# One block for the mixer and the output projection of a hybrid layer, on one Trainium2 core

## The reference, cut to what matters

```
y      = ssd_chunked(xs, dt, A, Bm, Cm) + d_skip * xs          # (512, 16, 64)
y_ssm  = rms_norm(y * silu(z), ssm_norm_w)                      # (512, 1024)
y_att  = rms_norm(forgetting_attention(q, k, v, log_f), attn_norm_w)
y_mix  = concatenate([y_ssm, y_att], axis=-1)                   # (512, 2048)
out    = einsum('bsk,kd->bsd', y_mix, w_out)                    # (512, 1024)
x      = layer_norm(ALPHA * x + (1 + g1) * out, ln1_g, ln1_b)
rms_norm(x, w): x * rsqrt(mean(x * x) + 1e-5) * w
```

## Time and profile before

| | us |
|---|---|
| runs | 2349.56, 2351.22, 2354.84 |
| profiled execution, span | 2351.2 |
| PE busy | 2251.0 (96%) |
| DVE busy | 879.8 (37%) |
| ACT busy | 645.8 (27%) |
| POOL busy | 267.2 (11%) |
| mixer, step 8 (from its first logits to the last values' end) | 454.3 to 480.4 |
| out, first product to the last transposes' end | 483.9 to 609.5 |

### The profile page before, as it was taken

The page is one execution under the profiler, slowest core; times in us unless marked ns, Lnnn a source line. Parts: engine busy times, 40 slices in busy tenths (PEclk is TensorE's granted clock), DMA queues, the critical chain, the costliest instruction groups (busy, mean ns, idle before and its releaser), DMA issues. The chain is left out here.

```text
span 2351.2 us, 27139 instructions
## 1 busy us (share of the span) xinstructions
PE 2251.0 (96%) x9635; PEld 1072.1 (46%) x9636; DVE 879.8 (37%) x1610; ACT 645.8 (27%) x849; POOL 267.2 (11%) x259
## 2 busy tenths in 40 slices
PE   6998999989899999989898999999999999999997
PEld 2444665544657576535545333333333333333332
DVE  1882666643444454533625111122111121111126
ACT  1211232221010000001301534444343543444440
POOL 4452111000000000000300000000000000000012
PEclk9999999989999999999896999999999999999999
DMA  8563312210722321141007869999999999999997
GB/s 325 205 198 82 88 56 100 99 54 1 303 72 82 133 72 72 54 140 61 1 27 283 355 273 392 422 423 410 422 422 417 423 413 420 422 409 422 423 412 299
DMA packets 139445, 569.43 MB, mean 242 GB/s; under 512 B 12311, under 2 KB 47308, under 8 KB 88172
## 3 DMA queue, kind: packets, MB, share of 16 engines
q1 hardware_dynamic: 123584, 527.89, 56.6%
q0 software_dynamic: 6272, 20.62, 2.2%
q10 hardware_dynamic: 9516, 19.99, 2.2%
HBM read 544.53 MB, written 23.92 MB: 242 GB/s over the span
## 5 line engine op out<-in xcount | busy, mean ns | idle before, releaser
L2564 PE MATMUL banks<-expert_ring,slot_token_gate 128*64 128x512 f32 x2880 | 636.7, 594 | 5.1 <-DMA expert_ring<-in_w_up_dram 3.0
L2564 PEld LDWEIGHTS banks<-expert_ring,slot_token_gate 128*64 128x64 f32 x2880 | 202.3, 137 | 399.9 <-issue 387.0
L2500 ACT COPY expert_ring<-expert_ring 128x2048 f32 x176 | 324.4, 1896 | 74.6 <-DMA expert_ring<-in_w_gate_dram 63.2
L2564 PE MATMUL banks<-expert_ring,slot_xT_gate 128*64 128x512 f32 x1440 | 329.5, 600 | 1.6 <-issue 0.9
L2564 PEld LDWEIGHTS banks<-expert_ring,slot_xT_gate 128*64 128x64 f32 x1440 | 100.5, 138 | 189.3 <-issue 181.9
L2677 DVE TENSOR_SCALAR col_onehot<-banks,slot_gates 128x512 f32<-128x512 f32 x45 | 33.8, 751 | 402.6 <-PE banks L2564 402.5
L521 PE MATMUL banks<-hT,weight_ring 128*128 128x512 f32 x320 | 141.2, 600 | 4.1 <-DMA weight_ring<-in_w_in_dram 3.2
L2662 DVE TENSOR_TENSOR slot_token_gate<-banks,expert_bias_T 128x512 f32<-128x512 f32 x45 | 31.1, 692 | 297.6 <-PE banks L2534 296.6
L1419 PE MATMUL banks<-hT,weight_ring 128*128 128x256 f32 x512 | 114.2, 383 | 4.7 <-PEq L2786 3.8
L1135 PE MATMUL banks<-weight_ring,mix_scaled 128*128 128x512 f32 x256 | 113.7, 606 | 3.5 <-DVE mix_scaled L1173 3.5
L785 PE MATMUL banks<-hT,weight_ring 128*128 128x512 f32 x256 | 116.1, 603 | 0.0
(11 more groups left out here) (455 smaller groups left out, 2520.0 us busy)
## 6 DMA issues: line engine op xcount, KB each, us to landing
expert_ring<-in_w_gate_dram SPq DMA_DIRECT2D x128, 1024.0 KB, 14.7
expert_ring<-in_w_up_dram SPq DMA_DIRECT2D x128, 1024.0 KB, 13.1
expert_ring<-in_w_down_dram SPq DMA_DIRECT2D x128, 1024.0 KB, 11.6
weight_ring<-in_w_ada_dram SPq DMA_DIRECT2D x12, 2048.0 KB, 10.6
weight_ring<-in_w_in_dram SPq DMA_DIRECT2D x8, 2048.0 KB, 11.6
weight_ring<-in_w_ff_in_dram SPq DMA_DIRECT2D x8, 2048.0 KB, 10.8
weight_ring<-in_w_ff_out_dram SPq DMA_DIRECT2D x8, 2048.0 KB, 13.2
weight_ring<-in_w_in_dram SPq DMA_DIRECT2D x24, 512.0 KB, 6.0
```

Source lines behind the costliest of these rows:

```text
L2500: nc.scalar.copy(flat_ring[:, c * size:(c + 1) * size], flat_ring[:, bass.ds(source + c * size, size)])\
L2564: x = nc.tensor.matmul(ps[h * CAP:(h + 1) * CAP, bank, :], lhs[:, k % 4, (k // 4) * CAP:(k // 4 + 1) * CAP], X.ring[:, m, k, h * HALF:(h + ...
```

## The change

The stages mixer and out become one block. The class OutProjection holds what stage_out did; stage_mixer calls its parts.

- The norm weights are multiplied into the rows of the output weights, in the ring, by POOL (weigh_rows, four operations of 128x1024 for each load): loads 0, 1, 2 behind POOL's scan work of steps 5, 6, 7, load 3 in step 8. mix_scaled is gone; PE multiplies mixT itself.
- ACT writes the squares into four buffers that lie in xbcT, POOL adds them (add_squares): the SSM half in step 8, the attention half behind it. There are two square_sums, in banks 6 and 4.
- PE does the SSM half's products in step 8, where the projections would stand: tile 0 in two pieces around values(6) and behind logits(58); then the SSM half's square_sums; tile 1's two halves behind logits(60) and logits(62), the second behind a wait for ss_read; tile 2 around values(7), tile 3 behind it. The attention half's products follow.
- x is loaded into the tile X, which now exists before the mixer and lends its space to the scan's acsb, dm, ctd, xc and xcd; SP issues it behind the last output weights. The layer norm's rows are loaded into xbcT when all squares are added. The ffn's first two weights are asked for when the SSM half's products are done.
- DVE does the SSM half of all four tiles first, then the attention half with the layer norm. The transposes of all tiles go through banks 4 and 7, so each waits for the copies of the tile before.

```diff
+class OutProjection:
+    SSM = [(0, 1), (5, 6), (2, 3), (0, 1)]
+    ATT = [(5, 6), (2, 3), (0, 1), (5, 6)]
+    TURN = (4, 7)
+    SUM_BANK = (6, 4)
...
+    def sync(self, sp):
+        for t in range(T):
+            sp.dma_start(G.X[:, t, :], self.A["x"][0, t * P:(t + 1) * P, :]).then_inc(self.x_in, 16)
+        G.W.upto(sp, G.W.index[("up", 0, 0)])
+        sp.wait_ge(self.sq_added, 2 * (KB - 1))
+        self.ln.load(sp)
+        G.W.upto(sp, G.W.index[("up", 0, 0)] + RING)
+    def weigh_rows(self, pool, q):
+        G.W.wait(pool, ("out", q))
+        w = G.W.view(("out", q))
+        for k in range(4):
+            b = R_SSMW + 4 * q + k
+            self.nc.gpsimd.tensor_scalar(w[:, k, :], w[:, k, :], G.pcol[:, b:b + 1], None, ALU.mult).then_inc(self.w_ok, 1)
+    def add_squares(self, pool, m):
+        n, total = (KB - 1) * m, self.total[m]
+        for b in range(1, KB):
+            pool.wait_ge(self.sq_ok, KB * m + b + 1)
...
+            self.nc.gpsimd.tensor_tensor(total, self.square[0] if b == 1 else total, self.square[b % 4], ALU.add)\
+                .then_inc(self.sq_added, 1)
+    def rest(self, pe):
+        def turn_x(t):
+            pe.wait_ge(self.ln.ready, t + 1)
+            if t:
+                pe.wait_ge(self.h_ok, KB * t)
...
+        pe.wait_ge(self.a_done, T)
+        nc.tensor.nop().then_inc(G.W.used, 2)
+        pe.wait_ge(self.ssm_read, 2)
+        self.att(pe, 0)
+        pe.wait_ge(self.ssm_read, 3)
+        self.att(pe, 1)
+        pe.wait_ge(self.ss_read, 2)
+        turn_x(0)
+        pe.wait_ge(self.ssm_read, 4)
+        self.att(pe, 2)
+        turn_x(1)
+        pe.wait_ge(self.y_read, 1)
+        self.att(pe, 3)
...
+        turn_x(2)
+        turn_x(3)
...
 (stage_mixer, gpsimd)
             for j in range(PAIRS):
                 ssm(j)
+                if j >= PAIRS - 3:
+                    out.weigh_rows(pool, j - (PAIRS - 3))
+            out.add_squares(pool, 0)
+            out.weigh_rows(pool, 3)
+            out.add_squares(pool, 1)
 (stage_mixer, tensor: step 8 is the one without "new")
                     proj(j, 0, depth=range(0, KB // 2))
+                else:
+                    pe.wait_ge(q["proj_read"], 3 * PAIRS - 1)
+                    out.ssm(pe, 0, 0, range(0, KB // 2))
...
+                    out.ssm(pe, 0, 1)
+                    pe.wait_ge(q["y_read"], PAIRS)
+                    out.square_sums(pe, 0)
...
+                    pe.wait_ge(q["state_ready"], PAIRS)
+                    out.ssm(pe, 1, 0)
...
+                    pe.wait_ge(out.ss_read, 1)
+                    out.ssm(pe, 1, 1)
...
+            pe.wait_ge(q["logits_read"], PAIRS * UNITS)
+            out.ssm(pe, 2, 0)
             values(PAIRS - 1)
+            out.ssm(pe, 2, 1)
+            pe.wait_ge(out.ssm_read, 1)
+            out.ssm(pe, 3, 0)
+            out.ssm(pe, 3, 1)
+            out.square_sums(pe, 1)
+            pe.wait_ge(q["pv_read"], PAIRS)
+            out.rest(pe)
 (stage_mixer, vector, end of each step)
                     turned(U + 4)
                     softmax(U + 6)
+                    if not new:
+                        out.mean_square(dve, 0)
                     turned(U + 6)
+            out.finish(dve)
```

More of the change, by code:

```diff
@@ L648, in stage_mixer @@
         st = sb("att_stats", [P, 3, 4])
[L649 to L653, removed]
+        acsb, dm, ctd = (G.X[:, t, :].rearrange("p (h n) -> p h n", n=P) for t in range(3))
+        xc, xcd = (G.X[:, 3, h * HALF:(h + 1) * HALF].rearrange("p (h w) -> p h w", w=HEAD) for h in range(2))
         bt = sb("b_tok", [P, P])
@@ L662, in stage_mixer @@
         acs_in = sem("acs_in")
+        out = OutProjection(nc, ctx, A, G)
         block = ctx.enter_context(nc.Block())
@@ L681, in _ @@
                 G.W.upto(sp, G.W.index[("qkv", 0)] + RING + j + 1)
+            for x in ("dm_sub", "eacs_ready", "y_done", "s_done"):
+                sp.wait_ge(q[x], PAIRS)
+            out.sync(sp)
         @block.gpsimd
@@ L756, in _ @@
                     proj(j, 0)
+                else:
+                    act.wait_ge(q["ssm_out"], PAIRS)
+                    out.squares(act, 0, range(0, 4))
                 if old:
@@ L762, in _ @@
                     proj(j, 1)
+                else:
+                    out.squares(act, 0, range(4, KB))
                 if old:
@@ L769, in _ @@
                     proj(j, 2)
+            out.root(act, 0)
+            act.wait_ge(q["pv_read"], PAIRS - 1)
+            out.squares(act, 1, range(0, KB - 1))
             values_read(PAIRS - 1)
+            act.wait_ge(q["pv_read"], PAIRS)
+            out.squares(act, 1, range(KB - 1, KB))
+            out.root(act, 1)
+            out.columns(act)
         @block.tensor
@@ L879, in _ @@
                     proj(j, 0, depth=range(KB // 2, KB))
+                else:
+                    out.ssm(pe, 0, 0, range(KB // 2, KB))
                 if old:
@@ L885, in _ @@
                     proj(j, 1)
+                else:
+                    pe.wait_ge(q["proj_read"], 3 * PAIRS)
+                    out.ssm(pe, 0, 1)
+                    pe.wait_ge(q["y_read"], PAIRS)
+                    out.square_sums(pe, 0)
                 if old:
```

375 lines of the change are left out of this document (180 added, 195 removed).

## The result

| | runs | median us | lowest to highest | ratio to before |
|---|---|---|---|---|
| before, same chip | 4 | 2352.34 | 2349.56 to 2354.84 | |
| changed kernel | 4 | 2340.97 | 2335.80 to 2341.84 | 0.9948 [0.9932, 0.9964] |
| before, chip of the second set | 11 | 2347.91 | 2345.81 to 2353.65 | |
| changed kernel, second set of runs | 7 | 2337.54 | 2334.49 to 2344.26 | 0.9957 [0.9942, 0.9973] |

The change takes off 0.52 and 0.43%, 11.4 and 10.4 us by the medians. On the second chip one more run of the kernel before took 3383.18 us at a granted clock of 0.65, and it is left out of the row above. The forecast was 2342.0 in a range of 2334 to 2350: the time is as foretold.

The account below looks back on a forecast made before the run. PE bounds the kernel (busy 2251.0 of 2351.2 us), so only its idle and slow-clock time can go: -21.6 + 4.1 + 0.8 + 3.7 + 3.1 + 0.45 + 0.3 = -9.15, giving 2342.0 us, range 2334 to 2350.

Parts of the forecast that it names:

- the idle time and slow clock of step 8: From step 8's first logits to turn_x(2): 21.6 us of 145.4 to be had, the most the change can take out.
- PE's own work: PE's work from step 8's first logits to turn_x(2), at the full clock: 123.8 us.
- (a): Steps 5 to 7: POOL's weighing holds DVE's scalings and delays PE's transposes, 4.1 us added in all.
- (b): Step 8, square_sums(0): PE waits for ACT's squares and POOL's adds, 0.8 us, bounds 0 and 5.
- (c): Step 8, before tile 1's second half: PE waits for ss_read, as mean_square stands behind the last softmax, 3.7 us.
- (d): Step 8: the clock falls in the 3.7 us gap and slows products, 3.1 us, bounds 0 and 6.
- (e): Block's end: turn_x(3) waits for tile 2's copies, 0.45 us; 54 semaphore clears where out had 22, 0.3 us.
- the first rival: Weighing holds nothing critical and the single gap does not lower the clock: -16.35, 2334.9 us; chance 0.22.
- gaps in steps 5 to 7 lower the clock: Rival: the gaps in steps 5 to 7 also lower the clock, 3.1 us each: +0.15, 2351.4 us; chance 0.17.
- The slower case: Rival: in steps 5 to 7 POOL's weighing holds DVE for its whole length: +18.55, 2369.8 us; chance 0.11.
- signs of being right: Step 8 gap near 3.7 us, then clock dip; steps 5 to 7 scalings over 2 us, gaps; turn_x(2) some 10 earlier.

Follow-up runs that it names:

- the version without the two gaps: Changed kernel with mean_square(0) ahead of the last softmax, square_sums(0) behind the logits of 60, and semaphore clears spread over five engines: 2323.82 us.
- four tensor_tensor: Changed kernel with each load weighed by four tensor_tensor of 128x1024 in place of four tensor_scalar: 2338.39 us, ratio 0.995.
- the one long weighing: Changed kernel with each load weighed by one tensor_tensor of 128x4096 in place of four tensor_scalar of 128x1024: 2351.63 us, ratio 1.0.
- the clears: Changed kernel with each of five engines clearing a fifth of the semaphores at every stage's end, in place of SP all: 2331.44 us, ratio 0.9925.
- the changed kernel again: Changed kernel with nothing edited, run once more on the second set's chip: median 2337.54 us.

## Why the prediction was right, and where it was not

**The mechanism was right.** What was to be had was the idle time and slow clock of step 8, 21.6 us, and the filling takes most of it: without it the stretch is 13.2 longer. PE's own work was put at 123.8; the version without the two gaps needs 124.4 with its 0.3 before turn_x(2).

**(a) The weighing, +4.1: the step that failed.** It cost nothing: from its first transposes to step 8's, step 7 takes 33.03 us in both kernels (421.18 to 454.21; before 420.24 to 453.27), steps 5 and 6 33.67 each in both. POOL's and DVE's timelines in step 7 of the changed kernel, against the earlier trace rows; the second line of POOL is the third of the four operations:

```profile
435.91 11.45 POOL L724 TENSOR_SCALAR weight_ring<-weight_ring,param_cols 128x1024 f32<-128x1024 f32 x4
441.61 2.84 POOL L724 TENSOR_SCALAR weight_ring<-weight_ring,param_cols 128x1024 f32<-128x1024 f32 x1
```

```profile
434.82 1.28 DVE L1223 TENSOR_SCALAR probs<-probs,att_stats 128x256 f32<-128x256 f32 x1
...
436.20 1.02 DVE L1223 TENSOR_SCALAR probs<-probs,att_stats 128x256 f32<-128x256 f32 x1
...
443.49 1.18 DVE L1223 TENSOR_SCALAR probs<-probs,att_stats 128x384 f32<-128x384 f32 x1
...
444.76 1.08 DVE L1223 TENSOR_SCALAR probs<-probs,att_stats 128x384 f32<-128x384 f32 x1
```

The weighing's length was right (11.4 foretold). Two things were not. First, the size of the hold. It was taken from L699, a tensor_tensor, and put on a tensor_scalar: the scaling of 436.20 ended at 437.22, in the midst of a weighing that ran from 435.91 to some 438.8, and in the three steps none that met a weighing alone took over 1.2 us (those of up to 2.2 us stood behind the scan's tensor_tensor). The pair of 443.49 and 444.76 was done at 445.84, 24.7 us into the step, 1.2 later than before; 447.6 was foretold, 3.9 later than before. Second, the delay was carried 3.0 us on to the step's last scaling. In the kernel before, DVE waits for PE behind this pair and behind the pair ahead of it:

```profile
439.59 0.88 DVE L940 COPY probs_T<-banks 128x128 f32<-128x128 f32 x4 [2.40 <-PE banks L821]
...
447.78 1.28 DVE L940 COPY probs_T<-banks 128x128 f32<-128x128 f32 x6 [1.01 <-PE banks L821]
...
449.33 0.69 DVE L917 CUSTOM_DVE_ANT_0 probs<-banks,key_bias 128x512 f32<-128x512 f32 x1 [0.27 <-PE banks L810]
```

The 1.01 and 0.27 took up the 1.2, and the last two scalings begin 31.05 and 31.9 us into the step in both kernels, and with four tensor_tensor too. Which of the two errors would have been enough by itself is not shown: no run has this pair 3.9 us late, and that would be more than the 1.3 of waiting.

The Trainium skill ("SBUF — State Buffer", section "SBUF: two separate sides") has the shared port pair locked for an instruction's whole length. Both tensor_tensor experiments agree: 6.91 us held beside 7.07, and an end 0.2 behind POOL's. POOL's tensor_scalar does not, and here the measurement decides: it lets DVE in midway. In steps 5 to 8 of the changed kernel's two profiles, scalings that began 0.3 to 0.6 us into a weighing ended 1.3 to 1.4 us into it; those that began 1.0 to 1.7 us in took 0.42, as they do alone; the three that began 1.9 us in or later ended 0.2 behind its end, as that of 443.49 did behind the weighing of 441.61. An example of the middle kind, POOL's row and then DVE's in step 5:

```profile
375.83 2.85 POOL L724 TENSOR_SCALAR weight_ring<-weight_ring,param_cols 128x1024 f32<-128x1024 f32 x1
```

```profile
377.26 0.42 DVE L1223 TENSOR_SCALAR probs<-probs,att_stats 128x384 f32<-128x384 f32 x1
```

Why it opens there is not shown.

**(b) square_sums(0), +0.8:** 1.14, in its place and by its releaser. **(c) ss_read, +3.7:** 3.42, likewise. Both terms hold. Moving mean_square on DVE and the square sums on PE takes them away, which the prediction did not see as a choice.

**(d) The clock behind that gap, +3.1:** a size, and not one number. Behind the same 3.42 us, 16 products took 7.13, 8.56, 8.83, 8.58 and 10.02 in five profiles (the changed kernel, the one long weighing, the clears, the four tensor_tensor, the changed kernel again), where 7.08 is the full clock: 0 to 2.9 us, three of them near 1.6. The 3.1 is the upper end. The gap of 1.14, which the prediction took to have no such price, cost 1.7 in three of the seven profiles that have it (8.76, 8.78, 8.78).

**(e) The end:** turn_x(3) at 0.45 came out at 0.07; the clears at 0.3 cost 1.9, outside the bounds of 0 and 1. The 3.78 of before was read as a fixed price, while 2.2 of it lay behind the last copy and grew with the number of semaphores.

**Why the number fits.** -9.15 was foretold and -14.2 came in the profiled execution: (a) gives -4.1, (d) -3.1, the end +1.6, all else +0.5. That is nearer to the first rival (-16.35), and its mechanism, nothing critical held and the clock up, is what this profile shows; the second profile, with 2.9 lost behind the gap, lies between the two. The total came near the forecast for two more reasons. The span 2351.2 was taken for that execution's time, which by the 1.8 us above was about 2353.0 (an estimate). And the medians scatter with the second mixer's course by some 6 us, so no run can tell -9 from -14 here; the stretch in the trace can. That 2340.97 lies so near to 2342.0 is thus luck in part: the filling was foretold rightly, the terms (a) and (d) were not in this profile.

**The rivals.** That gaps in steps 5 to 7 lower the clock was not seen in the changed kernel, as there were none; with one operation a load, gaps of 2.78 and 3.75 us there did. The slower case did not come: with four operations a load PE lost nothing, far from the 4.4 us a step from which it decides. With one operation a load it did, by 5.5 to 6.0 in two steps. Of the signs of being right, the gap ended by DVE's rms came; the dip of the clock behind it and the gaps in steps 5 to 7 did not, and the scalings of over 2 us in steps 5 and 6 stand behind the scan's tensor_tensor, not behind a weighing.

## What to carry to other kernels

Where an engine has nothing to put between small dependent steps, move independent work there: it pays twice, for the idle time and for the clock (here 7.4 and 8.7 us of PE's stretch). When one engine's work holds another, follow the held engine's row to the next place where it waits anyway before charging the delay to the end. In the trace of the result, look for what releases each new gap: here two waits were a matter of order and one of a row of clears on one engine. With all three mended the time is 2323.82 us, against 2337.54 and 2347.91 on one chip; 9.7 us stand in the traces at the places mended (4.9 in the stretch, 2.4, 0.7 and 1.8 at three stage ends).

## What was not expected of the hardware

- POOL's tensor_tensor was the faster one: 128x1024 with a broadcast column took 1.87 us (7.49 / 4), tensor_scalar 2.86 (11.45 / 4). As one operation of 128x4096 it took 7.07.
- POOL's tensor_tensor held DVE's scalings to its end. Its tensor_scalar of 2.86 us held them in about its first and its last microsecond and let them run between.
- One gap, two clocks: 3.42 us in step 8 cost 0 to 2.9 us, 1.14 us cost 0 or 1.7, and behind 2.37 us in the second mixer that mixer took about 6 us more or not, by execution of one kernel.
- The meeting at a stage's end took 4.1 us with 54 semaphores cleared by one engine and 2.2 with 22.
